# Merging stage of an encoder layer: y in two f16 parts, turned by a transposing DMA two tiles ahead, and a product that signals each half

## What is computed

```python
y = concatenate([y_h, y_a]).reshape(B, L, 2, 512)
y = rms_norm(y, out_norm.reshape(2, 512)).reshape(B, L, 1024)   # one scale for each half of a row
x = x + y @ w_out                                               # 1024 x 1024
x = x + ec_moe(rms_norm(x, mlp_norm), w_router, w_gate, w_up, w_down)
```

## Time and profile before

| | us |
|---|---|
| runs | 2716.11, 2723.81, 2722.59 (median 2722.59) |
| profiled execution | 2716.53, span 2714.7 |
| the merging stage in the span | 1711.2 to about 2003 |
| busy over the span: TensorE, VectorE, ScalarE, GpSimd | 2479.3, 1905.9, 1647.3, 1144.4 |

### The profile page before, as it was taken

The page is one execution under the profiler, slowest core; times in us unless marked ns, Lnnn a source line. Parts: engine busy times, 40 slices in busy tenths (PEclk is TensorE's granted clock), DMA queues, the critical chain, the costliest instruction groups (busy, mean ns, idle before and its releaser), DMA issues. The chain is left out here.

```text
span 2714.7 us, 51042 instructions
## 1 busy us (share of the span) xinstructions
PE 2479.3 (91%) x20059; PEld 1387.5 (51%) x20059; DVE 1905.9 (70%) x2642; ACT 1647.3 (61%) x2326; POOL 1144.4 (42%) x1032
## 2 busy tenths in 40 slices
PE   6899999879999999998898989799954899999997
PEld 4455555426666666663332233354533566666664
DVE  5446767647777777777898989566646577777773
ACT  6634455338888888887655855343434666676651
POOL 1224444226666666667303900244312355444531
PEclk9999999959999999998999989899965899999999
DMA  7413345344411212026796888655543899999972
GB/s 189 129 35 122 115 140 172 117 85 153 114 40 42 47 40 48 25 52 206 256 329 215 292 282 307 198 157 172 156 147 106 263 265 283 264 261 260 275 190 51
DMA packets 392346, 448.05 MB, mean 165 GB/s; under 512 B 205454, under 2 KB 270478, under 8 KB 389840
## 3 DMA queue, kind: packets, MB, share of 16 engines
q1 hardware_dynamic: 367632, 372.73, 45.0%
q0 software_dynamic: 12288, 38.05, 5.9%
q10 hardware_dynamic: 12224, 34.48, 3.7%
HBM read 270.67 MB, written 137.91 MB: 151 GB/s over the span
## 5 line engine op out<-in xcount | busy, mean ns | idle before, releaser
L1254 POOL TENSOR_TENSOR at_p<-at_pf,at_p 128x512 f16<-128x512 f32 x325 | 378.6, 1173 | 263.3 <-ACT at_p L1389 262.9
L1530 DVE TENSOR_REDUCE at_mxs<-at_pM 128x1 f32<-128x512 f32 x512 | 343.9, 688 | 104.6 <-PE at_pM L1420 102.7
L1388 ACT ACTIVATE at_pf<-at_pS,at_scale 128x1024 f32<-128x1024 f32 x260 | 289.8, 1115 | 110.2 <-PE at_pS L1451 105.6
L1389 ACT ACTIVATE at_p<-at_pS,at_scale 128x1024 f16<-128x1024 f32 x260 | 287.8, 1107 | 0.0
L1476 PE MATMUL at_pO<-at_vv,at_p 128*128 128x65 f16 x2080 | 227.0, 194 | 3.1 <-POOL at_p L1254 3.1
L1477 PE MATMUL at_pO<-at_vv,at_p 128*128 128x64 f16 x2080 | 226.4, 195 | 0.0
L1479 PE MATMUL at_pO<-at_vv,at_p 128*128 128x65 f16 x2080 | 225.8, 193 | 0.0
L1420 PE MATMUL at_pM<-at_kT,at_qT 96*128 96x512 f16 x512 | 200.1, 393 | 15.7 <-DMA at_qT<-s_QK 12.5
L1477 PEld LDWEIGHTS at_pO<-at_vv,at_p 128*128 128x128 f16 x2080 | 195.2, 98 | 37.5 <-issue 1.1
L1476 PEld LDWEIGHTS at_pO<-at_vv,at_p 128*128 128x128 f16 x2080 | 195.3, 97 | 35.0 <-issue 3.3
L1449 PE MATMUL at_pS<-at_qT,at_kT 97*128 97x512 f16 (+1 forms) x528 | 202.0, 383 | 3.4 <-DMA at_qT<-at_nmx 2.2
(11 more groups left out here) (423 smaller groups left out, 6237.5 us busy)
## 6 DMA issues: line engine op xcount, KB each, us to landing
sp_rows<-s_F SPq DMA_DIRECT2D x76, 512.0 KB, 5.6
s_F<-fs_a SPq DMA_DIRECT2D x72, 512.0 KB, 3.2
mo_raw<-in_w_gate SPq DMA_DIRECT2D x32, 1024.0 KB
mo_raw<-in_w_up SPq DMA_DIRECT2D x32, 1024.0 KB
mo_down<-in_w_down SPq DMA_DIRECT2D x32, 1024.0 KB, 4.9
s_QK<-pj_R ACTq DMA_DIRECT2D x18, 1024.0 KB, 3.9
s_G<-sp_gg SPq DMA_DIRECT2D x72, 256.0 KB, 4.2
sp_tab<-tab_spec SPq DMA_DIRECT2D x76, 224.0 KB, 4.0
```

The source lines that it names most:

```text
L1254: eng.tensor_tensor(p2[r][:, half, :], pf[:, r, half, :], p1[r][:, half, :], ALU.subtract).then_inc(own_done if own(g, half) else others_d ...
L1388: act.activation(pf[:, r, :, :], pS[g % 2][:, :, :], ACT.Exp, scale=scale[:, 0:1])
L1389: act.activation(p1[r][:, :, :], pS[g % 2][:, :, :], ACT.Exp, scale=scale[:, 0:1]).then_inc(p_made, 1)
L1530: dve.tensor_reduce(mxs[:, j // NC, j % NC:j % NC + 1], pM[j % 2][:, :], AX.X, ALU.max).then_inc(pM_free, 1)
```

## The change

`norm_y`, `turn_y`, `copy_yT` and the PSUM tile pY are removed. The scale ry now holds the factor 1024 (Y_SCALE) too. ScalarE `high_y` writes the high part y * ry as f16, VectorE `leave_y` the low part y * ry - high, both in rows of tokens (y_parts). SP `turn_y` turns both parts at once by one transposing DMA of 128x2048 f16 into y_both, which holds yT and yL. It is issued for tile t+2 when y_low(t+2) and the product of tile t are done. The product of a tile signals each half of its columns; `add` and the next product wait for halves. All five programs are reordered (sp, pool, act, pe and dve are SP, GpSimd, ScalarE, TensorE and VectorE):

```diff
+            def turn_y(t):
+                sp.wait_ge(y_low, 2 * t + 2)
+                if t >= 2:
+                    sp.wait_ge(produced, 2 * t - 2)
+                sp.dma_start_transpose(y_both[t % 2][:, :, :], y_parts[t % 2][:, :, :].rearrange("p m d -> p (m d)")
+                                       ).then_inc(y_turned[t % 2], 16)
+            for t in range(2):
+                load_g(t)
+                load_a(t)
             for i in range(PIECES):
...
-                    load_g(1)
-                    load_a(1)
-            load_g(2)
-            for t in range(2):
-                load_x(t)
+                    load_g(2)
+            turn_y(0)
+            load_x(0)
+            turn_y(1)
+            sp.dma_start(eye[:, :], io["tab_eye"]).then_inc(eye_in, 16)
+            load_x(1)
...
                     load_g(t + 3)
                 if t + 2 < NT:
-                    sp.wait_ge(y_normed, 2 * t + 2)
+                    sp.wait_ge(y_low, 2 * t + 2)
                     load_a(t + 2)
+                    turn_y(t + 2)
                 sp.wait_ge(added, 2 * t + 2)
...
             bias_z(0)
+            bias_z(1)
             of_y(0)
-            bias_z(1)
-            for t in range(NT):
-                if t + 1 < NT:
-                    of_y(t + 1)
+            bias_z(2)
+            of_y(1)
+            for t in range(NT + 1):
+                if t == 1:
+                    scale_x()
+                if t:
+                    of_x(t - 1)
                 if t + 2 < NT:
-                    bias_z(t + 2)
+                    of_y(t + 2)
+                if t + 3 < NT:
+                    bias_z(t + 3)
                 if t:
                     low_x(t - 1)
...
+            def high_y(t):
+                b = t % 2
+                act.wait_ge(root_y, t + 1)
                 if t >= 2:
-                    act.wait_ge(produced, t - 1)
+                    act.wait_ge(y_turned[b], 16 * (t // 2))
                 for h in range(2):
+                    act.activation(y_parts[b][:, 0, h * DH:(h + 1) * DH], y[:, b, h * DH:(h + 1) * DH], ACT.Copy,
+                                   scale=ry[:, b, h:h + 1]).then_inc(y_high, 1)
...
+                if i == 2:
+                    high_y(0)
+                    square_y(1)
+                if i == 5:
+                    high_y(1)
+            for t in range(NT + 1):
...
+                if t:
+                    square_x(t - 1)
+                if t + 2 < NT:
+                    square_y(t + 2)
+                if t:
+                    high_x(t - 1)
+                if t + 2 < NT:
+                    high_y(t + 2)
+                if t:
+                    copy_xT(t - 1)
+                    copy_logits(t - 1)
+                    store_x(t - 1)
...
+            def produce(t, h, pieces):
+                if pieces.start == 0:
+                    pe.wait_ge(y_turned[t % 2], 16 * (t // 2) + 16)
+                    pe.wait_ge(added, 2 * t + h - 1)
+                for k in pieces:
+                    last = product(t, k, h)
+                if pieces.stop == KD:
+                    last.then_inc(produced, 1)
...
             invert(0)
+            invert(1)
+            invert(2)
+            first_product()
             pe.wait_ge(eye_in, 16)
+            for t in range(1, NT):
+                if t + 2 < NT:
                     invert(t + 2)
+                produce(t, 0, range(KD))
+                produce(t, 1, range(0, KD // 2))
+                turn_x(t - 1)
+                produce(t, 1, range(KD // 2, KD))
+                route(t - 1)
...
+            def leave_y(t):
                 b = t % 2
                 for h in range(2):
+                    half = slice(h * DH, (h + 1) * DH)
+                    dve.wait_ge(y_high, 2 * t + h + 1)
+                    dve.scalar_tensor_tensor(y_parts[b][:, 1, half], y[:, b, half], ry[:, b, h:h + 1], y_parts[b][:, 0, half],
+                                             ALU.mult, ALU.subtract).then_inc(y_low, 1)
...
+                    dve.wait_ge(produced, 2 * t + h + 1)
...
+            close(1)
+            for i in range(PIECES):
                 low_w(i)
+                if i == 1:
+                    leave_y(0)
                 if i == 4:
+                    leave_y(1)
             for t in range(NT):
-                if t + 1 < NT:
-                    norm_y(t + 1)
                 if t + 2 < NT:
                     close(t + 2)
+                if t:
+                    norm_x(t - 1)
+                if t + 2 < NT:
+                    leave_y(t + 2)
                 add(t)
-                if t + 1 < NT:
-                    leave_y(t + 1)
-                norm_x(t)
+            norm_x(NT - 1)
```

More of the change, by code:

```diff
@@ L2228, in merge @@
         inverted, chain, biased = sem("inverted"), sem("chain"), sem("biased")
-        squared, eps_y, root_y, y_normed = sem("squared"), sem("eps_y"), sem("root_y"), sem("y_normed")
-        y_turned, yT_ready, produced, added = sem("y_turned"), sem("yT_ready"), sem("produced"), sem("added")
+        squared, eps_y, root_y = sem("squared"), sem("eps_y"), sem("root_y")
+        y_high, y_low, produced, added = sem("y_high"), sem("y_low"), sem("produced"), sem("added")
+        y_turned = [sem(f"y_turned{b}") for b in range(2)]
         x_squared, eps_x, root_x, x_normed = sem("x_squared"), sem("eps_x"), sem("root_x"), sem("x_normed")
@@ L2313, in of_y @@
                 if t >= 2:
-                    pool.wait_ge(y_normed, 2 * t - 2)
-                pool.tensor_tensor(mye[:, b, :], my[:, b, :], eps[:, :], ALU.add).then_inc(eps_y, 1)
+                    pool.wait_ge(y_low, 2 * t - 2)
+                pool.tensor_tensor(mye[:, b, :], my[:, b, :], eps_of_y[:, :], ALU.add).then_inc(eps_y, 1)
                 pool.wait_ge(eps_y, t + 1)
@@ L2368, in square_y @@
                     act.wait_ge(squared, 2 * t)
-                    act.wait_ge(x_squared, t - 1)
                 if t >= 2:
+                    act.wait_ge(x_squared, t - 2)
                     act.wait_ge(root_y, t - 1)
@@ L2373, in square_y @@
                     act.activation(junk[:, h * DH:(h + 1) * DH], y[:, b, h * DH:(h + 1) * DH], ACT.Square,
-                                   scale=DH ** -0.5, accum_out=my[:, b, h:h + 1]).then_inc(squared, 1)
-            def copy_yT(t):
-                act.wait_ge(y_turned, t + 1)
+                                   scale=DH ** -0.5 / Y_SCALE, accum_out=my[:, b, h:h + 1]).then_inc(squared, 1)
+            def high_y(t):
+                b = t % 2
+                act.wait_ge(root_y, t + 1)
                 if t >= 2:
-                    act.wait_ge(produced, t - 1)
+                    act.wait_ge(y_turned[b], 16 * (t // 2))
                 for h in range(2):
-                    act.activation(yT[t % 2][:, 4 * h:4 * h + 4, :], pY[:, 4 * h:4 * h + 4, :], ACT.Copy, scale=Y_SCALE
-                                   ).then_inc(yT_ready, 1)
+                    act.activation(y_parts[b][:, 0, h * DH:(h + 1) * DH], y[:, b, h * DH:(h + 1) * DH], ACT.Copy,
+                                   scale=ry[:, b, h:h + 1]).then_inc(y_high, 1)
             def copy_xT(t):
@@ L2416, in square_x @@
                 act.wait_ge(added, 2 * t + 2)
-                act.wait_ge(squared, 2 * min(t + 2, NT))
+                act.wait_ge(squared, 2 * min(t + 3, NT))
                 if t:
@@ L2457, in _ @@
                                    ).then_inc(x_sized, 1)
[L2458 to L2462, removed]
+                    act.wait_ge(x_sized, 1)
+                if t:
[10 more added lines that the diff above has]
+                    store_x(t - 1)
             act.wait_ge(lg_ready, NT)
@@ L2478, in invert @@
                 last.then_inc(inverted, 1)
[L2480 to L2486, removed]
             def turn_x(t):
@@ L2509, in route @@
                 last.then_inc(routed, 1)
[L2511 to L2524, removed]
@@ L2526, in _, with product, first_product @@
-            pe.wait_ge(consts, 4)
+            def product(t, k, h):
+                for x, w in ((yT, wH), (yT, wL), (yL, wH)):
+                    last = pe.matmul(pU[:, h * 512:(h + 1) * 512], x[t % 2][:, k, :], w[2 * k + h],
+                                     start=(k == 0 and x is yT and w is wH), stop=(k == KD - 1 and x is yL))
+                return last
+            def first_product():
+                pe.wait_ge(y_turned[0], 16)
+                for k in range(KD):
+                    for h in range(2):
+                        pe.wait_ge(wL_made, 2 * k + h + 1)
+                        last = product(0, k, h)
+                last.then_inc(produced, 2)
```

76 lines of the change are left out of this document (14 added, 62 removed).

## The result

| | us |
|---|---|
| before, this comparison | median 2719.7 of 4 runs (2716.1 to 2723.8) |
| after | median 2806.5 of 4 runs (2804.6 to 2807.0) |
| ratio | 1.0327 [1.0302, 1.0352] |
| profiled executions, span | 2714.7 before, 2804.8 after |
| merging stage, first load of mg_gin to first load of the next stage | 292.7 before (1711.2 to 2003.9), 389.2 after (1700.2 to 2089.4) |

The kernel is 3.3% slower, 27 us above the forecast time of 2780, inside the range. The stage is 96.5 us longer where +60.8 was forecast. The span grew by 90.1: the stage began 11.0 us earlier, and what follows it took 715.4 us where it had taken 710.8. I don't put these two differences down to the change: a version whose code ahead of the stage is the same began it at 1698.8, another at 1712.7, and what follows the stage took 709.7 to 714.5 us in the nine versions tried.

A forecast was written before the change was run, and what follows sets the result against it. The prediction took the ring through SP's load of y to bound the merging stage: 17.6 us plus 0.8 for the transposing DMA, a period of 18.4, +61 us on 2716.5, half of 6 added: 2780, range 2743 to 2824.

The forecast's parts named there:

- The ring: Merging stage: add(t-1), SP, load_a landing, square_y, of_y, high_y, leave_y, add(t) form a closed wait of 17.6 us; 80%.
- a hidden ring: Rival, merging stage: load latency stays hidden, TensorE bounds at 13.0 us a tile, -26 us, 2694; 9%.
- the forecast's break-even of 14.4: Merging stage: period at which the change neither gains nor loses, with load_a landed 7.0 us after add.
- end of leave_y to landed load (add, SP, burst, transposing DMA): Ring terms: add 1.4 us, end of add to landed load_a 11.0, transposing DMA +0.8.
- squares and of_y: Ring term: from square_y's start to of_y's end, on the loaded y, 2.9 us.
- high_y and leave_y: Ring term: high_y 2 x 0.72, second half of leave_y 0.75, hand-overs 0.1, together 2.3 us.
- The transposing DMA: SP's queue: turn_y's own latency is covered; its place ahead of load_a adds 0.8 us to the period.
- The rival by the Trainium skill's figure: Sixteen serial 128x128 blocks take 20.9 us of DMA a tile, load_a lands 16.5 us later, time near 3030; 1%.
- The sum: Merging stage: leave_y(2) ends at 1749.5, plus 276.0 for 15 rounds, -2.8, +25.4, giving 2048.1, so +61 us.
- rows 4: Profile rows of the kernel before that the prediction read for when SP's loads land, 5.4 (median) to 9.8 us (longest).
- TensorE inside the period: TensorE idles some 4 us before route; the lower clock costs some 2 us, which fit in the period, costed at nothing.
- The halves: Signalling the product's halves by themselves gives nothing while add(t) is held by leave_y.

The follow-up runs named there:

- the version with the early load: Kernel after, with SP alone issuing load_a of y one tile earlier, for t+3 ahead of turn_y(t+2): 2695.5 us, ratio 0.994.
- two others: Early load plus one product signal for both halves, 2699.4 us; early load plus ScalarE's sum of mgain squares moved behind high_y(2), 2691.0 us.
- with its opening put in order: Early load, plus mgain's squares moved behind high_y(2) and the x_scale store moved to SP's last round: 2684.9 us, ratio 0.9912.

## Why the prediction was right, and where its sizes were off

**The ring.** Right, with every joint in the timeline, and proved by its removal: one load issued earlier takes the period from 20.4 to 13.0 us and the time from +3.3% to -0.6%. The forecast rested on one comparison, 9.9 to 11.4 us from add to a landed load against the 6.4 that a hidden ring would allow; the run with load_a first after add shows how the balance runs: with less queue ahead of it the period is 14.8, just beyond the forecast's break-even of 14.4.

**Its terms,** for the round 1887.26 to 1907.83:

| term | forecast | measured |
|---|---|---|
| end of leave_y to landed load (add, SP, burst, transposing DMA) | 13.2 | 13.9 |
| squares and of_y | 2.9 | 2.4 |
| high_y and leave_y | 2.3 | 4.3 |
| period | 18.4 | 20.6 |

The mis-sized term is leave_y: **0.75 us a half forecast, 1.76 measured**. Two halves, and then GpSimd's low_x (ns, least/median/most; first and last start):

```profile
L2582 DVE SCALAR_TENSOR_TENSOR mg_y_parts<-mg_y,mg_ry,mg_y_parts x2: 991/1800/2610, 1904.3 to 1905.2; 128x512 f16<-128x512 f32 x2
...
L2346 POOL TENSOR_TENSOR hy_norm<-mg_xn,hy_norm x1: 2574/2574/2574, 1904.7 to 1904.7; 128x1024 f16<-128x1024 f32 x1
```

The second half starts at 1905.2, inside low_x, and ends 0.55 us after low_x does. I had priced it by low_w, the same instruction form. Where GpSimd is idle, as at tile 1 in the opening, leave_y does cost just that, 1.41 us for both halves (the version with the early load):

```profile
1718.15 1.41 DVE L2584 SCALAR_TENSOR_TENSOR mg_y_parts<-mg_y,mg_ry,mg_y_parts 128x512 f16<-128x512 f32 x2 [0.75 <-ACT mg_y_parts L2399]
```

So neither the f16 output nor the SBUF operands by themselves make it slow. It took 1.65 where its first half ran beside the end of GpSimd's bias_z, and 3.52 with low_x as well. The row nearest in place was in the trace of the kernel before, and I had not read it:

```profile
1868.36 3.75 DVE L2568 TENSOR_SCALAR mg_yn<-mg_y,mg_ry 128x512 f32<-128x512 f32 x2 [0.87 <-POOL mg_ry L2317]
1869.52 2.31 POOL L2333 TENSOR_TENSOR hy_norm<-mg_xn,hy_norm 128x1024 f16<-128x1024 f32 x1
```

norm_y stood where leave_y now stands, right behind of_y and beside bias_z and low_x, and took 3.75 us for two halves. The new leave_y reads SBUF where the old one read PSUM, and the old one took 0.68 a half beside no low_x. A rule of the Trainium skill says this ahead of any run: SBUF — State Buffer, section "SBUF: two separate sides", has VectorE, where it reads two SBUF inputs, and a GpSimd instruction that reads SBUF exclude each other for a whole instruction, whichever starts first. The trace agrees: leave_y and low_x take 3.52 and 2.57 us together, 1.65 and 2.13 in the run that keeps them apart. With the row of norm_y for two halves the period would have come out at 18.4 + 2.2 = 20.6.

**The transposing DMA.** 0.8 us a round forecast, 2.3 by the experiment. It held SP for 3.6 us from SBUF, where the loads of attention took 2.14 from memory. Of the 3.6 us, 2.3 showed in the period; that the rest is covered by the burst, which has to drain anyway, is my reading and not shown by itself. The forecast's own terms also add up to an upper bound of 18.4 + 2.6 = 21.0, not 20.8. The DMA kept TensorE waiting once, 4.8 us ahead of product 0 in the opening, and never in the rounds of the ring: its landings were

```profile
DMA to landing us min/median/max: 4.3/6.5/7.7
```

The rival by the Trainium skill's figure (VectorE: DVE Perf Modes, "The three transpose paths": 16 blocks one behind the other, an estimated 20.9 us) is refuted by these 6.5.

**The sum.** 15 rounds: 273.2 forecast, 308.3 measured. Of the 35.1 us the first round has 6.6 (25.0 us long, its load landed after 10.2 us behind the small store; the 9.8 in rows 4 was the load in that very place, and I had used it for another), the 13 middle ones 2.0 each, 26.2, and the last 2.3. The middle rounds are 20.4 us, close to the upper bound of 20.8. The opening, from the start of the stage to the end of leave_y(2), was 0.9 longer (39.2 for 38.3; product 0 ended 4.7 us later in it than before and not 0.8, behind its wait for the transposing DMA, but leave_y(2) ended later still), the end 1.7 longer (27.1 for 25.4; the first 36 matmuls of product 16 took 10.82 us after a gap, 7.94 at full clock), the tail 2.0 shorter (14.6 for 16.6). Together 35.7, the difference between 96.5 and 60.8. Outside the stage 6.4 came back by the variation told at the top, which is luck, and 2.7 had been added to the forecast for the median: 35.7 - 6.4 - 2.7 = 26.6, and the measured median of 2806.5 lies 26.5 above 2780.

**TensorE inside the period.** Right: clock 0.83, invert 1.98 us, the first 36 matmuls of a product 9.05 for 7.94, all inside the wait. One row was off: a product starts 1.0 us after leave_y ends and not 2.2, since the longer leave_y leaves copy_xT and route the time to be done first. **The halves.** Right: worth nothing, neither on the kernel before nor with the early load in the steady state.

**The chances.** The hidden ring had 9% and rightly lost. Its size was about right: 26 us forecast for it, with 13.0 a tile; the version with the early load has 13.0 and a stage 17 us shorter, and with its opening put in order, 22 (26 by the medians, 2684.9 against 2710.9).

**What stays open.** Why the run with the early load alone had no round of 20 us while two others did. All three had the slow stretch behind the small store (35 GB/s from 1751 to 1753 in the early load's run), but the transposing DMA caught in it landed there after 8.5 us, in the others after 11.7 and 13.2. How such a store could hold the DMA engines is open too. That turn_x now stands in the middle of the product's second half was not tried by itself.

## What to carry to other kernels

When a step is moved earlier, follow its operand back through the queue that loads it: a load whose place was harmless becomes the bound the moment its first user comes a tile sooner, and issuing that load a round earlier decides between 3.3% loss and 0.6% gain. If what waits is an in-order queue as well as an engine, reordering the engine alone gains nothing. Price an instruction by the row that ran in the same place, with the same neighbours, not only by the row of the same form.

## What the hardware showed

- VectorE and GpSimd on SBUF: two passes of 128x512 by VectorE with two SBUF inputs took 1.41 us with GpSimd idle, 1.65 beside the end of a GpSimd pass of 128x512, and 3.52 with a GpSimd pass of 128x1024 as well, which took 2.57 for 2.13 itself.
- A transposing DMA of 128x2048 f16 from SBUF to SBUF holds SP's queue 1.8 to 4.6 us in the kernel after (up to 9.3 in other versions), against 0.47 for a plain load of 256 KB, and lands in 4.3 to 7.7 (up to 13.2).
- In ten of ten executions a store of 128 x 4 bytes was followed after 1 to 4 us by a stretch of 3 to 8 us mostly below 80 GB/s, and the 256 KB load issued right behind it landed in 9.1 to 11.6 us (nine executions), against 4.9 in the one version that issues the store elsewhere; that the store is the cause rests on this one version.
- TensorE with one gap of 5.1 us ahead of route in every round of 20.6 was granted 0.83 of its clock; without gaps, in the early load's version, 1.00.
